# Expert weight tiles of half the rows in full length, with a pipelined scan, a halved top-k, earlier loads and late norms, in a three-layer network in one kernel

## The reference

```python
def step(carry, inp):                    # mLSTM scan over chunks, 4 heads, two directions
    s = jnp.einsum('bhjd,bhsd->bhjs', qc, kc) * jnp.exp(logw - m[..., None])
    num = jnp.einsum('bhjs,bhsd->bhjd', s, vc) + dec[..., None] * jnp.einsum('bhjk,bhkv->bhjv', qc, c0)
    ...
    hc = num / jnp.maximum(jnp.abs(den), jnp.exp(-m))[..., None]
    c_new = dn[..., None, None] * c0 + jnp.einsum('bhs,bhsk,bhsv->bhkv', wa, kc, vc)
...
merged = gates[..., :D_MODEL] * y_f + gates[..., D_MODEL:] * y_m      # then @ w_out, + x
...
aff = jax.nn.softmax(jnp.einsum('bld,de->ble', h, w_router), axis=-1)
vals, idx = lax.top_k(jnp.swapaxes(aff, 1, 2), cap)                   # 16 experts, 128 of 1024 tokens each
xs = h[bidx, idx]
hid = silu(xs @ w_gate[e]) * (xs @ w_up[e])                           # each w: 1024 x 1024
y = (hid @ w_down[e]) * vals                                          # added to its tokens' rows
```

## Time and profile before

| | |
|---|---|
| time, median of 3 (lowest to highest) | 3307.52 us (3302.03 to 3307.57) |
| the profiled execution: time, span | 3307.75 us, 3305.9 us |
| TensorE matmul busy, of the span | 2930.8 us, 89% |
| TensorE weight load | 2081.0 us, 63% |
| VectorE | 1666.1 us, 50% |
| ScalarE | 1278.3 us, 39% |
| mean granted TensorE clock | 0.937 |
| chain that ended last | PE 80%, DVE 8%, ACT 5%, DMA 4% |
| DMA packets, bytes | 176664, 388.56 MB |
| DMA over the experts (1172 to 1790 us) | 334 GB/s |

### The profile page before, as it was taken

One profiled execution on the slowest core, in us unless ns is written; L12 is line 12 of the kernel. 1 busy time (PEld: TensorE's weight loads), 2 busy tenths in 40 slices (PEclk: granted clock), 3 DMA queues, 4 the chain that ended last, 5 costly groups with the idle time before them and its releaser, 6 DMA issues.

```text
span 3305.9 us, 37686 instructions
## 1 busy us (share of the span) xinstructions
PE 2930.8 (89%) x13860; PEld 2081.0 (63%) x13860; DVE 1666.1 (50%) x3240; ACT 1278.3 (39%) x2362; POOL 114.2 (3%) x154
## 2 busy tenths in 40 slices
PE   7999977899989179999996798799999978999999
PEld 3454456578868156776663575477667865776677
DVE  2127535334335866666662556743652446645523
ACT  2101222223314154554552545643652446535522
POOL 0000000000000001110010000000000000000000
PEclk9999978999989589999998899899999988999999
DMA  9420000022232469999997110020012020200121
GB/s 356 132 77 0 26 26 1 0 102 102 79 139 109 152 222 356 361 363 368 365 363 201 67 26 26 20 59 23 30 52 102 13 77 14 77 1 33 52 77 51
DMA packets 176664, 388.56 MB, mean 118 GB/s; under 512 B 7028, under 2 KB 8084, under 8 KB 176256
## 3 DMA queue, kind: packets, MB, share of 16 engines
q1 hardware_dynamic: 157920, 318.79, 27.6%
q0 software_dynamic: 18448, 67.72, 6.2%
q10 hardware_dynamic: 144, 0.01, 0.0%
HBM read 354.98 MB, written 31.51 MB: 117 GB/s over the span
## 4 chain that ended last, share of the span: by engine, by line
PE 80%; DVE 8%; ACT 5%; DMA 4%; issue 2%; SPq 1%; POOL 0%; DVEq 0%; POOLq 0%; ACTq 0%
PE psum L292 19%; PE psum L699 7%; PE psum L701 7%; PE psum L700 7%; PE psum L1215 4%; PE psum L1331 4%; PE psum L1217 4%; PE psum L1216 4%; PE psum L1349 3%; PE psum L1160 3%; PE psum L1159 3%; PE psum L1158 3%; PE psum L1378 2%; PE psum L1426 2%; PE psum L1428 2%
## 5 line engine op out<-in xcount | busy, mean ns | idle before, releaser
L700 PE MATMUL psum<-ring_r,kctx_r 128*128 128x512 f32 (+1 forms) x544 | 214.7, 395 | 0.0
L700 PE MATMUL psum<-ring_r,cols_r 128*128 128x512 f32 (+1 forms) x544 | 212.5, 391 | 0.0
L1746 ACT ACTIVATE ring<-ring,att 128x256 f32<-128x256 f32 (+7 forms) x256 | 173.1, 677 | 65.7 <-DVE att L2288 65.6
L1331 PE MATMUL psum<-wide 64*128 64x512 f32 (+2 forms) x704 | 158.6, 535 | 21.2 <-DVE att L2288 18.2
L292 PE MATMUL psum<-hidden,ring 128*128 128x512 f32 x384 | 167.4, 597 | 5.8 <-DVE wide L2045 3.8
L2157 DVE TENSOR_TENSOR ring_r<-ring,pair_r 128x1024 fp32r<-128x1024 f32 x128 | 148.0, 1218 | 23.8 <-ACT pair_r L1647 23.8
L1216 PE MATMUL psum<-ring_r,wide_r 128*128 128x512 f32 x384 | 151.3, 394 | 0.0
L1349 PE MATMUL psum<-ident,ring 128*128 128x128 f32 x640 | 122.3, 299 | 26.6 <-ACT sel_wT L1758 16.1
L1349 PEld LDWEIGHTS psum<-ident,ring 128*128 128x128 f32 x640 | 69.8, 145 | 106.8 <-issue 70.7
L292 PEld LDWEIGHTS psum<-hidden,ring 128*128 128x128 f32 x384 | 73.4, 192 | 96.7 <-issue 94.5
L699 PE MATMUL psum<-small_r,kctx_r 128*128 128x512 f32 (+1 forms) x240 | 101.1, 421 | 29.4 <-DVE ring_r L682 20.4
(11 more groups left out here) (447 smaller groups left out, 6842.4 us busy)
## 6 DMA issues: line engine op xcount, KB each, us to landing
ring<-in_w_gate SPq DMA_DIRECT2D x64, 1024.0 KB, 8.9
ring<-in_w_up SPq DMA_DIRECT2D x32, 1024.0 KB, 9.4
hidden<-in_w_up SPq DMA_DIRECT2D x32, 1024.0 KB, 9.1
hidden<-in_w_down SPq DMA_DIRECT2D x32, 1024.0 KB, 7.2
pair<-in_w_down SPq DMA_DIRECT2D x32, 1024.0 KB, 7.9
ring<-in_w_ada SPq DMA_DIRECT2D x24, 1024.0 KB, 12.0
ring<-in_w_in SPq DMA_DIRECT2D x24, 1024.0 KB, 7.3
ring<-in_even_w_in SPq DMA_DIRECT2D x16, 1024.0 KB, 15.7
```

Source lines behind the costliest of these rows:

```text
L700: self.eng.matmul(outp, XHIGH[b][:, k, :], low[:, k, 0:wd], start=False, stop=False)
L1331: mm = pe.matmul(bank(2 * (q % 2) + h)[:, 0:n], qT2[row, c, span(b)], kT2[row, 0 if name == "C" else c, k:k + n], start=True, stop=not dia ...
L1746: act.activation(sv, sv, ACT.Exp, bias=nmx[:, q:q + 1], scale=-1.0, accum_out=esum[:, r:r + 1]).then_inc(S(name + "_e"), 1)
```

## The change

Five edits.

1. **Scan.** Each engine's step is cut in two parts, and the second part of a step comes after the first part of the next. Scaling the carried part moves from VectorE to ScalarE (scan_carried) into two buffers obs; the additions are two for four heads; the PSUM banks are laid out anew.
2. **Merge.** The waits of TensorE for mg_mul and mg_add fall away; the first row block of mT is split before the last group's weights; POOL loads ga1 and x1 once the last branch product is done.
3. **Router.** Affinities lie as 32 rows of 512 (two halves for each expert). Each half yields its 128 largest in order; the halves are joined by comparing one list with the other reversed. The last replacement is left out.
4. **Layer border.** Both residual stores (xb, x3) go out by row block. The last two norms of N4 run inside the first iterations of cq, whose first operands are split under the last output product.
5. **Experts.** A tile holds 512 rows of a weight matrix in all 1024 columns, in place of 1024 rows in 512 columns. A product runs over four row groups k with both column halves m in turn, and both results end with the second tile. All waits for a half result (silu, hidden_of, output) wait for both; ScalarE's silu moves behind high(e,3).

```diff
@@ load
-                ms = slice((j % 2) * HALF, (j % 2 + 1) * HALF)
-                w = w[e, :, ms].rearrange("(k p) n -> p k n", p=P) if isinstance(e, int) else \
...
-                for k0 in (0, 4):
-                    sp.dma_start(MRAW[j][:, k0:k0 + 4, :], w[:, k0:k0 + 4, :])
+                rs = slice((j % 2) * HALF, (j % 2 + 1) * HALF)
+                w = w[e, rs, :].rearrange("(k p) n -> p k n", p=P) if isinstance(e, int) else \
...
+                for k0 in (0, 2):
+                    sp.dma_start(MRAW[j][:, k0:k0 + 2, :], w[:, k0:k0 + 2, :])
@@ POOL, merge
-            pool.wait_ge(S("mg_add"), 16)
+            pool.wait_ge(S("mg_br"), 32)
+            pool.dma_start(ga1b, scratch["ada"][2 * D:3 * D].partition_broadcast(P)).then_inc(S("ga1"), 16)
             for i in range(4):
                 pool.dma_start(x1[:, 2 * i:2 * i + 2, :], ...
-            pool.dma_start(ga1b, scratch["ada"][2 * D:3 * D].partition_broadcast(P)).then_inc(S("ga1"), 16)
+            pool.wait_ge(S("mg_add"), 16)
@@ TensorE, scan
-            for i, (d, c, has) in enumerate(steps):
+            def scan_first(i):
+                if i >= 1:
+                    pe.wait_ge(S("scan_kw"), 4 * i)
...
+            def scan_second(i):
+                if has:
+                    pe.wait_ge(S("scan_c"), 4 * (i - 1))
+                    if no >= 1:
+                        pe.wait_ge(S("scan_o"), no)
...
+                    pe.wait_ge(S("scan_se"), no + 1)
...
+                pe.wait_ge(S("scan_kw"), 4 * (i + 1))
+                if i >= 1:
+                    pe.wait_ge(S("scan_c"), 4 * i)
...
+            for i in range(len(steps) + 1):
+                if i < len(steps):
+                    scan_first(i)
+                if i >= 1:
+                    scan_second(i - 1)
@@ TensorE, experts
+                for p in range(PIECES):
+                    pe.wait_ge(S("mw_low"), moe_pieces(e, j) + (p + 1))
+                    k = PIECES * q + p
+                    for m in range(2):
+                        outp, ms = bank(2 * (j // 2) + m), slice(m * HALF, (m + 1) * HALF)
+                        high = MHIGH[q][p // 2][:, p % 2, ms]
+                        pe.matmul(outp, xh[:, k, :], high, start=(k == 0), stop=False)
+                        pe.matmul(outp, xh[:, k, :], low[:, p, ms], start=False, stop=False)
+                        mm = pe.matmul(outp, xl[:, k, :], high, start=False, stop=(k == KT - 1))
@@ down
-                for m in range(2):
-                    moe_full(pe, e, 4 + m)
-                    group(pe, bank(4 + m), [(hidT[:, k, :], MRAW[4 + m][:, k, :]) for k in range(KT)]).then_inc(S("moe_d"), 1)
+                for q in range(2):
+                    moe_full(pe, e, 4 + q)
+                    for p in range(PIECES):
+                        k = PIECES * q + p
+                        for m in range(2):
+                            mm = pe.matmul(bank(4 + m), hidT[:, k, :], MRAW[4 + q][:, p, m * HALF:(m + 1) * HALF],
+                                           start=(k == 0), stop=(k == KT - 1))
+                    mm.then_inc(S("moe_d"), 1)
@@ VectorE, output
-                dve.wait_ge(S("moe_d"), e * 2 + (m + 1))
+                dve.wait_ge(S("moe_d"), e * 2 + 2)
@@ VectorE, scan
+                    dve.wait_ge(S("scan_ob"), no + 1)
+                    dve.tensor_tensor(ob[:, 0:3, :], ob[:, 0:3, :], bank(4)[:, 0:3 * VW].rearrange("p (h n) -> p h n", h=3), ALU.add)
+                    dve.tensor_tensor(ob[:, 3, :], ob[:, 3, :], scan_u[3], ALU.add).then_inc(S("scan_o"), 1)
@@ VectorE, router
-            link(dve.tensor_copy(affT, psum[0:NEXP, HALF:3 * HALF]))
+            link(dve.tensor_copy(affT, bank(1)[0:2 * NEXP, :]))
...
-                link(dve.match_replace(affT, v, affT, -1.0))
-            dve.tensor_copy(idxf, idx).then_inc(S("topk"), 1)
+                if r < CAP // 8 - 1:
+                    link(dve.match_replace(affT, v, affT, -1.0))
+            link(dve.tensor_copy(idxf, idx))
+            link(dve.tensor_copy(valr, vals[:, ::-1]))
+            dve.tensor_copy(idxr, idxf[:, ::-1]).then_inc(S("topk"), 1)
...
+            link(dve.tensor_tensor(firsts, v0, v1, ALU.is_ge))
+            link(dve.tensor_tensor(valc, v0, v1, ALU.max))
+            link(dve.tensor_tensor(i0, i0, i1, ALU.subtract))
+            link(dve.scalar_tensor_tensor(i0, i0, float(HALF), firsts, ALU.subtract, ALU.mult))
+            dve.scalar_tensor_tensor(idxc, i1, float(HALF), i0, ALU.add, ALU.add).then_inc(S("route"), 1)
@@ layer border
-            dve.wait_ge(S("res1_out"), before("res1_out") + 16)
-            first_job(1)
-            qk_dve("cq", "ck")
+            qk_dve("cq", "ck", late=last_norms_dve)
...
+            def last_norms_pe(i):
+                if i < 2:
+                    N4.transposes(pe, TT - 2 + i)
+                    N4.done(pe, TT - 2 + i)
...
+                if i == 1:
+                    act.wait_ge(S("res1_out"), before("res1_out") + 16 * TT)
```

More of the change, by code:

```diff
@@ L712, in next_job, with out_rows @@
                     s.weights()
+        def out_rows(layer, j, t):
+            return (M2[layer] if j < 2 * TT else H2[1])[:, :, span(t)]
         def rows_of(keys):
@@ L727, in span, with heads3 @@
             return slice(c * P, (c + 1) * P)
+        def heads3(b, last):
+            return [bank(b)[:, h * VW:(h + 1) * VW] for h in range(3)] + [last]
+        scan_i = heads3(3, bank(5)[:, 0:VW])
+        scan_u = heads3(4, bank(5)[:, VW:2 * VW])
+        scan_d = heads3(6, bank(7)[:, 0:VW])
         def chain_row(d, h):
@@ L1555, in _, with scan_weigh @@
             act.wait_ge(S("c_zero"), 2)
-            for i, (d, c, has) in enumerate(steps):
+            def scan_weigh(i):
+                d, c, has = steps[i]
                 no = outs_before[i]
@@ L1599, in _ @@
                         sigmoid(c)
+                if t + 1 == len(PASSES):
+                    act.wait_ge(S("mg_add"), 14)
+                    s2.rows(mT[:, :, span(0)])
                 for p in range(4):
@@ L1607, in _ @@
             act.wait_ge(S("mg_add"), 16)
-            s2.rows(mT[:, :, span(0)])
             items = rows_of([("wo", m) for m in range(2)])
@@ L1819, in out_act @@
             def out_act(layer):
[L1820 to L1823 removed]
+                items = rows_of([("out", layer, m) for m in range(2)]) + ([] if layer else [("cq", 0)])
+                for i in range(2 * TT):
+                    next_job(s2, i, items, lambda t: out_rows(layer, i + 1, t))
                     i -= TT
@@ new lines, in scan_ends @@
+                dve.wait_ge(S("scan_o"), no + 1)
+                g0 = chain_row(d, 0)
+                link(dve.scalar_tensor_tensor(rec, ob[:, :, DH], -1.0, colv[:, c, 3, g0:g0 + NH], ALU.mult, ALU.max))
+                link(dve.tensor_tensor(rec, rec, ob[:, :, DH], ALU.max))
+                link(dve.reciprocal(rec, rec))
+                if no:
+                    dve.wait_ge(S("scan_out"), no)
+                hv = hsum[:, c - CT, :].rearrange("p (h n) -> p h n", h=NH)
+                first = not any(s[1] == c for s in steps[:i])
@@ new lines, in scan_ends @@
+                for h in range(NH):
+                    if first:
+                        ins = dve.tensor_scalar(hv[:, h, :], ob[:, h, 0:DH], rec[:, h:h + 1], None, ALU.mult)
+                    else:
+                        ins = dve.scalar_tensor_tensor(hv[:, h, :], ob[:, h, 0:DH], rec[:, h:h + 1], hv[:, h, :], ALU.mult, ALU.add)
+                ins.then_inc(S("scan_out"), 1)
+            for i in range(len(steps) + 1):
+                if i < len(steps):
+                    scan_scores(i)
+                if i >= 1:
+                    scan_ends(i - 1)
```

273 lines of the change are left out of this document (138 added, 135 removed).

## The result

The changed kernel took 3381.9 us (3370.67 to 3382.12, four runs) against 3307.55 us (3302.03 to 3312.31, four runs) of the kernel before: ratio 1.0217, interval 1.0191 to 1.0243. So it is slower, by about 2%, and I had forecast 3224 us.

A forecast was written before the change was run, and what follows sets the result against it. TensorE was taken as the bound nearly everywhere, though in the scan it took turns with VectorE. 3307.75 - 70 - 15 - 26 - 15 + 43 = 3224.75, stated as 3224 us, range 3190 to 3258.

The forecast's parts named there:

- Scan, -70: Scan over the chunks: pipelined steps become TensorE-bound at 5.7 us each, clock 0.97, saving 70 us.
- rival (c): Scan bound by handshakes between engines, not TensorE: 8 us a step instead of 5.7, total 3261 us; chance 0.14.
- Merge, -15: End of the merge: earlier gate load and first-block split let TensorE's second row block begin at 958.6, not 973.4; -15 us.
- Search, -26: Router's top-128 search: 32 rows of 512 columns cut a round from 3.9 to 2.3 us; -26 us.
- Border, -15: Layer border: TensorE's 16.75 us idle behind a store and a slow product go, less transposes and copy waits; -15 us.
- Experts, +43: Expert loop: late outputs make TensorE wait for subtractions (26 us) and gathers (17 us), plus 0.7 tail; +43 us.
- The wait for the first subtraction: Expert loop: TensorE's gate product waits 1.36 us a turn behind down for VectorE's first subtraction.
- The 0.5 us at the second tile: Expert loop: TensorE waits 0.5 us more a turn for the first subtraction of the second tile.
- Scatter to gather: Expert loop: time from scatter to gather stays 11.4 us, so the gather lands 1.3 us late in 13 turns, 17 us.
- Rival (d): Expert loop: TensorE's clock falls to 1.2 GHz behind the new waits, 6 us a turn, making the kernel slower; chance 0.03.
- Rival (a): Expert loop: the gather stays hidden because its latency falls in a longer loop, total 3207 us; chance 0.22.
- Packets of 4096 bytes have nothing to give here: Expert tiles: longer packets save nothing, since the stage is bound by TensorE, which no load delays.

The follow-up runs named there:

- the pair 3163.93 and 3167.29: Changed kernel with the low(e+1,0) subtractions moved ahead of output(e-1,0): 3163.93 us with 4096-byte packets, 3167.29 us with 2048-byte packets.
- the exchanged order: Changed kernel with two lines of VectorE's turn exchanged, the four low(e+1,0) subtractions ahead of output(e-1,0): 3163.93 us, ratio 0.9574.
- the old tiles: Kernel of edits 1 to 4 with the expert tiles as before, one wait changed so output(e-1,0) waits for all of down: 3390.22 us, ratio 1.0253.
- eleven breaks: Changed kernel with VectorE waiting for its own last signal between all subtractions of the second, third and fourth tile: 3251.95 us, ratio 0.9835.

## Why the prediction was wrong, step by step

**Scan, -70; measured -75.5.** The step was priced at 5.7 us and took 5.51, with the clock at 1.00 where I had taken 0.97. The fourth plain product started at 449.9, where I had put 456: 2.8 us of that because the first one already came earlier, and the rest because the fourth stood 3.8 us behind the third (446.07 to 449.86), where I had 6.1. The bound, TensorE, was right, and rival (c), 8 us a step, falls.

**Merge, -15; measured -15.3. Search, -26; measured -26.5.** Right in mechanism and size.

**Border, -15; measured -13.6** from the last output product to the third cq product (35.7 us before, 22.1 after). Right, but the first cq product does wait 3.32 us, for an addition behind VectorE's splitting, and it starts at half clock. The rest of the -21.1 behind the last scatter varies between the kernels: it took 1493.3 to 1505.6 us in the nine with edit 4, 1501.3 on the mean, and 1508.0, 1510.9 and 1514.4 in the three without, 1511.1 on the mean. So the changed kernel's own 1493.3 is the lowest of nine, and by the means edit 4 is worth some 10 us over that stretch. Edits 1 to 4 give 136 us by the run of their own, where the sum had 126.

**Experts, +43; measured +207.** The late outputs made 20.1 us of waits for subtractions, where I had 26, but 154.0 of waits for gathers, where I had 17, and 28 of half clock, where I had none. The wait for the first subtraction, priced at 1.36, measured 1.21. The 0.5 us at the second tile didn't come. The late outputs were placed well: the second ends 6.1 us after down (1290.82 - 1284.72), where I had 6.2; the scatter starts at 7.4, where I had 7.5. **The step that failed is the next one:** "Scatter to gather was 1521.17 - 1509.80 = 11.4 us", carried over as a constant. It was 1316.21 - 1292.13 = 24.1 us, 12.8 of them the held scatter. I had moved an instruction of GpSimd under a different stretch of VectorE and priced it by the old stretch. My own text had the two facts side by side: VectorE's queue behind down has 8.2 us of work without a break, and the scatter falls due in it. I asked only who waits for the scatter, not what the scatter itself waits for.

The trace before had the sign of it. Timeline of GpSimd before, two turns:

```profile
1519.79 0.53 POOL L864 COPY kctx<-kctx 128x1 int32 x1 [8.40 <-DMA scratch_acc<-wide,kctx]
...
1547.23 2.64 POOL L870 DMA_INDIRECT scratch_acc<-wide,kctx  x1 [0.87 <-issue]
```

The copy, 0.18 us elsewhere, ended at 1520.32, when VectorE's run of four subtractions ended; the scatter took 2.64 us in some turns and 1.59 in others. When a fixed piece of work takes two durations, the longer one holds some waiting. The least and the most of one line, not its median, would have shown it.

The Trainium skill (SBUF — State Buffer, section "Who interferes with whom") says that VectorE and GpSimd share one pair of ports under an exclusive lock, and that a VectorE instruction with two SBUF inputs contends with a GpSimd instruction that reads SBUF. By it a held GpSimd instruction would have been a rival of my forecast, and I hadn't looked it up. The traces agree for the index copy (0.18 against 13.71 us). They go beyond it in two ways: the same page infers that such an instruction leaves the making of descriptors alone, and here the scatter was held by 12.8 us; and it speaks of a lock held for one instruction, where here a row of ten or more subtractions of 1.22 us each kept GpSimd out to its end.

**The clock.** Rival (d) had the half level in every turn, at 6 us; it came in every turn at 2.2 us on the mean, and not behind the new waits of my forecast but behind the waits for the gather (11.3 to 12.6 us). At the short wait of 1.21 us the first product ran at once at full clock (0.50 and 0.40 us for its first matmuls). So (d) had a true part, and its cause was not the one that I named. "Slower than before" came true for another reason: the clock is 28 of the 206.6 us.

**The gather's latency.** Rival (a) said that the gather lands sooner in a longer loop. That part came true: 4.6 us (median) in place of 7.2. It couldn't hide the gather, which was issued 12.7 us later than I had reckoned (24.1 against 11.4 behind the scatter).

**Packets.** "Packets of 4096 bytes have nothing to give here" was right, by the pair 3163.93 and 3167.29. The wait of 0.7 us that I had worked out from the Trainium skill (DMA: Bandwidth & Descriptors, Queues, rings and completion order) for a gather beside longer packets stands beside 8.6 - 7.7 = 0.9 us measured in that pair. That the two are near is no test of the rule: the page's packet is typically a bundle of 9 to 17 descriptors, and I had taken a packet of the profile's rows, 2 or 4 KB, for one. It would not have changed the time, since the gather is hidden there; and in the changed kernel itself, where it is not hidden, it lands after 4.6 us. I put that down to its going out late in the turn, when most of the weights are there; the DMA share of 0.00 right behind its landing fits, and no run tests it.

**Open.** Why a run in which VectorE has just caught up with ScalarE lets GpSimd in between two subtractions (1.59 to 2.66 us before, 1.89 with low(e+1,0) first), and a run that has its operands waiting doesn't. In the rows it is a choice between two ends: the held scatter of 2.64 us (1547.23, before), that of the exchanged order and those with a wait or a memset all end 1.46 to 1.47 us behind the end of the first subtraction of VectorE's run, and in the changed kernel it is the same 1.46 us behind the last. That the next subtraction is already handed over before the last ends would explain both; no run here tests it.

## What to carry to other kernels

Before you move work of GpSimd, or lengthen a run of two-operand VectorE instructions, look at what VectorE does while GpSimd's instruction is due: here such a run added 12.8 us to a 1.6 us scatter, and TensorE stood still for 154 us behind it over the loop. If the run can't be moved, put a short instruction of another kind into it; the better cure is the order, here one exchange of two lines worth 218 us. And when a step's duration is carried over to a new place, ask first whether it was work or waiting, by the spread of its line.

## What the runs showed of the hardware

- Subtractions of 128x1024 float32 with both operands in SBUF, 1.22 us each and back to back, kept out GpSimd's index copy for 13.5 us and its scatter for 12.8 us. In all thirteen turns in which the scatter fell due inside such a run, it ended 1.46 to 1.49 us after the last of them, also with the old tiles (1.45 to 1.48). But four such subtractions in a row, whose rounded operands ScalarE delivers only just ahead of them, let the scatter in after the first (1.89 us, the exchanged order).
- A memset of 0.06 us between two of them let the scatter in (1.89 us), as did a wait of VectorE for its own last signal, at some 0.1 us of VectorE for each.
- A copy out of PSUM on VectorE didn't hold GpSimd: the index copy at 1291.08 ran in 0.18 us inside VectorE's copy from PSUM at 1290.73.
- Behind a wait of 11.6 us TensorE was granted 1.2 GHz for 6.1 us, behind one of 1.21 us it stayed at 2.4. With eleven breaks the waits for the gather were 2.5 to 4.2 us, and a part at 1.2 GHz came behind nine of thirteen.
